# Key pages one step sooner, sample sums and offsets inside the projection steps, value products behind them, in a two-layer hybrid decoder step

## The chip, the cores and the metric

The kernel is one program on one core of a Trainium2 chip, written with an instruction stream of its own for each engine: TensorE (PE, products and transposes into PSUM), VectorE (DVE), ScalarE (ACT), GpSimd (POOL) and SyncE (SP, which requests most transfers). The streams run in order and meet in semaphores. The metric is the device time of one execution in microseconds; smaller is better.

## What is computed

The reference runs one inference step of a two-layer decoder on a prompt group (1 x 256 tokens) and a sample group (8 x 4 tokens), 288 token columns in all, with shared float32 weights and a model width of 1024:

```python
for l in range(DEPTH):                       # 2 layers
    m = silu(c) @ cond_w + cond_b            # 9 vectors per sequence: shift, scale, gate
    x = post(0, x, swiglu(pre(0, x), ffn_w_in[0], ffn_w_out[0]), 0.5)
    x = post(1, x, mixer(pre(1, x), ...), 1.0)
    x = post(2, x, swiglu(pre(2, x), ffn_w_in[1], ffn_w_out[1]), 0.5)

def mixer(a, ...):
    gq, gk, gv, gg, glr, mu, mv, sq, sk, sv = split_cols(a @ w_in)   # one projection, 3088 columns
    o_gla = gated linear attention (gates from the low-rank glr @ w2), 4 heads
    o_gm  = chunked spatial gating of mu, mv, 4 heads
    z     = q @ k^T * HD ** -0.5 + bias      # stick-breaking attention, 8 heads of 64
    A     = exp(log_sigmoid(z) + suffix sums of -softplus(z)), masked
    o_sb  = A @ v                            # samples: 1024 past keys and values in 8 pages of 128, through page_table
    return concat(o_gla, o_gm, o_sb) @ w_out
```

New keys, values and recurrent states are outputs too.

## The kernel before, in words

**Stages.** Per layer: feed-forward 0 (22 input steps, 16 output steps), a seam (norms, gates, residual), the mixer, a seam, feed-forward 1, a seam. A weight step brings 1 MB into one of two buffers `raw`; ScalarE rounds it (`w_hi`, L1325), VectorE takes the difference (`w_lo`, L1712), and TensorE forms three products for each 128 x 128 block with the 288 token columns (L605 to L607). A step's split into `w_hi` and `w_lo` waits until TensorE is done with the step two before it.

**Conditioning.** `cond_w` comes in chunks through the four buffers `direct` (and `side`); `cond_products` multiplies it into PSUM banks 6 and 7 with sequences on the partitions. VectorE copies the sums to `crow` (`copy_sums`, `copy_wide`), TensorE turns them back (`cond_turn`, L655), and VectorE makes scales, shifts and gates out of them (`modulation`), waiting for `cond_t`.

**Mixer, projection steps.** `MIX_STEPS` lists the twelve steps j = 0 to 11 (queries in 0 and 1, keys in 3 and 4). Beside them runs the scoring of the samples' past keys: 16 key chunks of four pages (1 MB each), requested by SyncE into `direct`, turned in 32 x 32 blocks by VectorE (`turn_keys`, L1990, 2 chunks a step), multiplied with the samples' queries by TensorE (`key_chunk`, L911, two chunks behind each of the steps 3 to 10, by `KEYS_AT`). The queries for that are repeated (`qrep`), transposed by TensorE (L1000), and laid out by VectorE (`sample_queries`). ScalarE brings the scores into `z` (`scores`), in two groups of four samples. Then, for each group g: cap (`sample_cap`; for group 1 GpSimd, L2354 and L2356), exp and log (`sample_log1p_exp`), sums (`sample_sums`, with totals at L2013 and L2014), offsets by small products (`part_offsets`) and their subtraction (`sample_offsets`), exp (`sample_weights`), a transpose (`turn_weights`), `regroup` on TensorE (L934), a copy into `a_keys` (`weights_by_page`). The low-rank gate product (L1017 to L1019) stands behind step 4.

**Mixer, tail.** Behind step 11: prompt scores, row transposes of keys and values, gated linear attention, spatial gating, prompt sums, and 16 value chunks (`value_chunk`, L957), 8 for each group, four buffers deep: SyncE requests chunk n when chunk n - 4 is used. The order of all this is written out by hand in each engine's stream. Then comes the output projection (first products L667).

Of the kernel before, what the change touches and what calls it, by code (L numbers as in the profile page):

```python
# [24 lines left out]
ALU = mybir.AluOpType  # L25
# [22 lines left out]
def decoder_step(nc, x_prompt, x_sample, c_prompt, c_sample, cache_sb_k, cache_sb_v, state_gla,  # L48
# [40 lines left out]
    KEYS_AT = {j: (2 * j - 6, 2 * j - 5) for j in range(3, 11)}  # L89
# [25 lines left out]
    with ctx:  # L115
# [60 lines left out]
        w2 = tile("w2", [LR, GW])  # L176
# [13 lines left out]
        lr = tile("lr", [LR, T])  # L190
# [13 lines left out]
        crow = tile("crow", [P, NCH // 2 * P], F32, shared + (2 * FB + 4) * T * 4)  # L204
# [22 lines left out]
        lrw_hi = tile("lrw_hi", [P, KB, P], F32R, crow_end)  # L227
        lrw_lo = tile("lrw_lo", [P, KB, P], F32R, crow_end + KB * P * 4)
        at[0] = crow_end + 2 * KB * P * 4
        lr_raw = tile("lr_raw", [P, KB, LR])  # L230
        qb = tile("qb", [P, 4, 4 * PR, 8, TS], F32, at[0])
        S0 = tile("S0", [P, B, GP, HD])
        att = tile("att", [P, 2, PT_, GP, P])
# [26 lines left out]
        direct_used = signal("direct_used", ND, 4 + NC0 + NSIDE)  # L260
        pages_in = signal("pages_in")
# [19 lines left out]
        cond_t = signal("cond_t", 3, 1)  # L281
# [23 lines left out]
        lrw_round = signal("lrw_round")  # L305
        lrw_ready = signal("lrw_ready")
# [98 lines left out]
        ROWS = 7  # L405
        TOKEN_BANKS = ((2, 3), (6, 7), (4, 0))
# [9 lines left out]
        def _(sp):  # L416
# [62 lines left out]
            def page_chunk(l, cache, dp, first, n, wait):  # L479

# [3 lines left out]
                room(l, dp, wait)  # L484
                for t, page in enumerate(found):
                    src = cache[l, ds(page, 1), :, :, :].rearrange("o s h d -> s (o h d)")
                    sp.dma_start(direct[:, n % 4, 512 * t:512 * t + 512], src).then_inc(direct_in[n % 4].sem, 16)  # L487

            def key_chunks(l, *chunks):
                for n in chunks:  # L490
                    page_chunk(l, cache_sb_k, DP_K, 4 * n, n, n)
# [58 lines left out]
            for l in range(L):  # L550
# [8 lines left out]
                mix_in(2, 3)  # L559
                key_chunks(l, 0, 1)  # L560
                mix_in(4)
                key_chunks(l, 2, 3)
                mix_in(5)
                for j in range(3, 9):
                    mix_in(j + 3)
                    key_chunks(l, *(n + 4 for n in KEYS_AT[j]))
                for n in range(NPC):
                    if n == 4:
                        for s in range(2):
                            mix(l, mix_w_out, POS_MO, s, s, s * 256)  # L570
                    page_chunk(l, cache_sb_v, DP_V, 4 * n, n, n)
# [26 lines left out]
        def _(pe):  # L598
# [11 lines left out]
            cond_sums = PS[:, 6:8, :].rearrange("p a b -> p (a b)")  # L610

# [116 lines left out]
            def ffn(l, n, cond_in):  # L728
# [32 lines left out]
                for s in range(N_IN - 4, N_IN):  # L761
                    in_step(l, n, s, s % 2)
                    if s == N_IN - 3:
                        turn_sums()
# [1667 lines left out]
```

## Time and profile before

| | |
|---|---|
| Time, median of 3 runs | 1382.98 us (1381.0 to 1384.24) |
| Profiled execution | time 1380.02 us, span 1378.3 us, mean granted clock 0.988 |
| TensorE busy | 1324.4 us, 96% |
| VectorE, ScalarE, GpSimd busy | 795.5 us (58%), 585.6 us (42%), 81.5 us (6%) |
| Read from HBM | 317.93 MB, 234 GB/s over the span |

The stretches of layer 0 are, in us from the start of the span: feed-forward 0 from 37 to 267, seam to 288, projection steps to 384, tail to 444, output projection to 472, seam to 486, feed-forward 1 to 706. Layer 1 follows with the mixer from 957 to 1114. Busy times overlap; an engine that isn't the bottleneck may idle at no cost.

### The profile page before, as it was taken

The page shows a single profiled execution, that of the slowest core. Times are in us where ns is not written, and L with a number is a line of the kernel's source. Part 1 is how long each engine was busy: PE and PEld are TensorE (multiplying, and loading weights), DVE is VectorE, ACT ScalarE, POOL GpSimd, SP SyncE. Part 2 cuts the span into 40 slices and gives each one's busy share as a digit, 9 for nine tenths or more (in the row PEclk, how much of TensorE's full clock was granted, in tenths as well). Part 3 has the DMA queues.
Part 4 walks back from the last instruction along what each step waited for, and adds up shares of the span by engine and source line. Part 5 has one row for each costly group of instructions (what it writes and reads, how often), then busy time and mean ns, then how long its engine had stood idle before and what let it go on. Part 6 is the DMA issues. An engine that isn't in the chain of part 4 may idle for free.

```text
span 1378.3 us, 34467 instructions
## 1 busy us (share of the span) xinstructions
PE 1324.4 (96%) x14014; PEld 1267.4 (92%) x14014; DVE 795.5 (58%) x1162; ACT 585.6 (42%) x965; POOL 81.5 (6%) x153
## 2 busy tenths in 40 slices
PE   6899999999989999999999999999998998999998
PEld 5899999999976899999989999998997787999998
DVE  2555553667884655554465555447788657555544
ACT  2532333443565543334353333345346555333343
POOL 4000000010040000000000000002003100000000
PEclk9999999999999999999999999999999998999999
DMA  9878779789989894658975566996997993565453
GB/s 330 266 231 259 219 244 311 219 257 327 298 274 343 256 324 140 168 154 270 282 239 156 161 174 195 289 276 199 329 342 228 338 326 101 156 174 158 136 168 97
DMA packets 423815, 324.49 MB, mean 235 GB/s; under 512 B 15559, under 2 KB 351719, under 8 KB 423696
## 3 DMA queue, kind: packets, MB, share of 16 engines
q1 hardware_dynamic: 421124, 317.03, 75.5%
q0 software_dynamic: 2272, 5.61, 1.2%
q8 instruction: 90, 1.47, 0.4%
q14 instruction: 29, 0.24, 0.1%
q10 hardware_dynamic: 300, 0.13, 0.0%
HBM read 317.93 MB, written 4.78 MB: 234 GB/s over the span
## 4 chain that ended last, share of the span: by engine, by line
PE 84%; DVE 5%; DMA 4%; SPq 3%; ACT 2%; issue 1%; DVEq 1%; POOL 0%; ACTq 0%
PE PS L605 23%; PE PS L607 23%; PE PS L606 23%; PE PS L633 3%; SPq L487 2%; PE PS L911 2%; PE PS L667 1%; PE PS L668 1%; PE PS L669 1%; DMA direct<-in_cond_w 1%; DMA direct<-in_cache_sb_v 1%; PE PS L957 1%; SPq L454 1%; DMA raw<-in_ffn_w_in 1%; DMA raw<-in_mix_w_in 1%
## 5 line engine op out<-in xcount | busy, mean ns | idle before, releaser
L1712 DVE TENSOR_TENSOR w_lo<-raw,w_hi 128x1024 fp32r<-128x1024 f32 (+1 forms) x368 | 392.9, 1106 | 445.9 <-ACT w_hi L1325 445.4
L1325 ACT ACTIVATE w_hi<-raw 128x1024 fp32r<-128x1024 f32 (+1 forms) x368 | 337.7, 960 | 657.6 <-PE PS L607 573.5
L605 PE MATMUL PS<-a_hi,w_hi 128*128 128x288 f32 x1760 | 524.0, 298 | 0.2 <-issue 0.2
L606 PE MATMUL PS<-a_lo,w_hi 128*128 128x288 f32 x1760 | 519.2, 295 | 0.0
L607 PE MATMUL PS<-a_hi,w_lo 128*128 128x288 f32 x1760 | 517.6, 294 | 0.0
L605 PEld LDWEIGHTS PS<-a_hi,w_hi 128*128 128x128 f32 x1760 | 329.7, 187 | 3.6 <-issue 3.3
L607 PEld LDWEIGHTS PS<-a_hi,w_lo 128*128 128x128 f32 x1760 | 331.4, 188 | 0.0
L606 PEld LDWEIGHTS PS<-a_lo,w_hi 128*128 128x128 f32 x1760 | 330.4, 188 | 0.5 <-issue 0.3
L606 PE MATMUL PS<-h_lo,w_hi 128*128 128x288 f32 x704 | 208.4, 296 | 0.0
L605 PE MATMUL PS<-h_hi,w_hi 128*128 128x288 f32 x704 | 208.1, 296 | 0.0
L607 PE MATMUL PS<-h_hi,w_lo 128*128 128x288 f32 x704 | 208.0, 296 | 0.0
L605 PEld LDWEIGHTS PS<-h_hi,w_hi 128*128 128x128 f32 x704 | 133.7, 190 | 0.4 <-issue 0.4
L607 PEld LDWEIGHTS PS<-h_hi,w_lo 128*128 128x128 f32 x704 | 132.0, 188 | 0.0
L606 PEld LDWEIGHTS PS<-h_lo,w_hi 128*128 128x128 f32 x704 | 131.9, 187 | 0.0
L633 PE MATMUL PS<-direct,cT 128*32 128x128 f32 x1920 | 66.0, 290 | 8.8 <-DMA direct<-in_cond_w 4.8
L1990 DVE STREAM_TRANSPOSE direct<-direct 128x2048 f32<-128x2048 f32 x32 | 72.2, 2289 | 0.0
L633 PEld LDWEIGHTS PS<-direct,cT 128*32 128x32 f32 x1920 | 55.1, 117 | 14.9 <-DMA direct<-in_cond_w 6.5
L2331 POOL TENSOR_TENSOR X<-X,Y 128x576 f32<-128x576 f32 x10 | 14.0, 1415 | 758.7 <-DVE Y L1798 758.7
L667 PE MATMUL PS<-a_hi,w_hi 128*128 128x288 f32 x160 | 50.0, 313 | 5.6 <-DVE a_lo L1961 5.6
L668 PE MATMUL PS<-a_lo,w_hi 128*128 128x288 f32 x160 | 48.1, 301 | 0.0
L669 PE MATMUL PS<-a_hi,w_lo 128*128 128x288 f32 x160 | 48.1, 300 | 0.0
L1863 DVE TENSOR_TENSOR h_lo<-hf,h_hi 128x288 f32 (+1 forms) x88 | 40.3, 458 | 11.7 <-issue 9.6
(327 smaller groups left out, 1160.1 us busy)
## 6 DMA issues: line engine op xcount, KB each, us to landing
raw<-in_ffn_w_in SPq DMA_DIRECT2D x176, 512.0 KB, 5.0
direct<-in_cond_w SPq DMA_DIRECT2D x240, 256.0 KB, 5.0
direct<-in_cache_sb_k SPq DMA_DIRECT2D x128, 256.0 KB, 4.4
direct<-in_cache_sb_v SPq DMA_DIRECT2D x128, 256.0 KB, 4.4
raw<-in_ffn_w_out SPq DMA_DIRECT2D x64, 384.0 KB, 3.8
raw<-in_mix_w_in SPq DMA_DIRECT2D x48, 512.0 KB, 6.9
raw<-in_ffn_w_out SPq DMA_DIRECT2D x64, 320.0 KB, 4.5
side<-in_cond_w SPq DMA_DIRECT2D x48, 256.0 KB, 5.3
```

Of the source, the lines that this page charges most:

```text
L487: sp.dma_start(direct[:, n % 4, 512 * t:512 * t + 512], src).then_inc(direct_in[n % 4].sem, 16)
L605: pe.matmul(out, whi, hi, start=begins and i == 0, stop=False)
L606: pe.matmul(out, whi, lo, start=False, stop=False)
L607: last = pe.matmul(out, wlo, hi, start=False, stop=ends and i == n - 1)
L633: last = pe.matmul(PS[32 * g:32 * g + 32, 6 + pair, c * P:c * P + P], cT[:, 4 * half + kb, :], rows[:, kb * 512 + g * P:kb * 512 + g * P + P],
L667: pe.matmul(out, whi, a_hi[:, k, :], start=k == 0, stop=False)
L668: pe.matmul(out, whi, a_lo[:, k, :], start=False, stop=False)
L669: last = pe.matmul(out, wlo, a_hi[:, k, :], start=False, stop=k == KB - 1)
L1325: act.activation(w_hi[:, s, at_:at_ + n], raw[:, s, at_:at_ + n], ACT.Copy)\
L1712: tt(w_lo[:, s, at_:at_ + n], raw[:, s, at_:at_ + n], w_hi[:, s, at_:at_ + n], ALU.subtract).then_inc(lo_done.sem, 1)
L1863: tt(h_lo[:, at_, :], hf[:, s:s + 1, :], h_hi[:, at_, :], ALU.subtract)\
L1990: dve.transpose(direct[:, n % 4, :], direct[:, n % 4, :]).then_inc(k_turned.sem, 1)
```

## The change

It has five parts. (1) Key chunks are requested, turned and multiplied one step sooner: chunks 0 and 1 stand behind step 2 and the last two behind step 9. The query transposes move between the two halves of step 2. (2) Sums of group 0 move from step 10 to step 8, its offsets to steps 9 and 10, its weights' transpose and the regrouping to step 11; the sums of group 1 come right behind the gate's scan, its offsets earlier too. ScalarE and TensorE do key rows inside steps 10 and 11. (3) Value chunks 0 to 7 each stand earlier in TensorE's stream, and every fifth one (`n % 5 == 4`) uses a new buffer `extra`. `S0` and `att` move onto parts of `Fm` and of the split buffers that are free by then; the load of `S0` waits for the last reads of the queries and keys there, and the seam for the state's output. (4) The products of `cond_w` take their columns in another order, so that VectorE's 32 x 32 transposes out of PSUM give the turned sums in `sums` directly; `crow`, `cond_turn`, `cond_t` and TensorE's waits for `mod_ready` go, and VectorE's loop over the first feed-forward's steps is unrolled. (5) The low-rank product takes unsplit weights of 32 columns in four column groups, summed by `w2`, repeated four times on the partitions.

```diff
-    KEYS_AT = {j: (2 * j - 6, 2 * j - 5) for j in range(3, 11)}
+    KEYS_AT = {j: (2 * j - 4, 2 * j - 3) for j in range(2, 10)}
...
+        extra = tile("extra", [P, 2048])
+        a_turn0 = tile("a_turn0", [P, 4 * NPG * 32], F32, at[0] - 8192)
+        S0 = tile("S0", [P, B, GP, HD], F32, shared + GQ * T * 4)
... sync
-                mix_in(2, 3)
+                mix_in(2)
                 key_chunks(l, 0, 1)
+                mix_in(3)
+                key_chunks(l, 2, 3)
                 mix_in(4)
-                key_chunks(l, 2, 3)
-                mix_in(5)
                 for j in range(3, 9):
-                    mix_in(j + 3)
-                    key_chunks(l, *(n + 4 for n in KEYS_AT[j]))
+                    mix_in(j + 2)
+                    key_chunks(l, 2 * j - 2, 2 * j - 1)
+                mix_in(11)
                 for n in range(NPC):
-                    if n == 4:
+                    if n % 5 == 4:
+                        extra_chunk(l, n)
+                    else:
+                        page_chunk(l, cache_sb_v, DP_V, 4 * n, n - (n + 1) // 5)
+                    if n == 3:
                         for s in range(2):
                             mix(l, mix_w_out, POS_MO, s, s, s * 256)
-                    page_chunk(l, cache_sb_v, DP_V, 4 * n, n, n)
... tensor
-                                         rows[:, kb * 512 + g * P:kb * 512 + g * P + P],
+                                         rows[:, kb * 512:kb * 512 + 512].rearrange("p (b g i) -> p g b i", g=4, i=32)[:, g],
...
-            def cond_turn(first=0, end=NCH // 2):
-
-                for q in range(first, end):
-                    last = pe.transpose(cond_sums[:, q * P:q * P + P], crow[:, q * P:q * P + P], ident[:, :])
-                last.then_inc(cond_t.sem, 1)
...
                             last = products(PS[:, 2 * s + h, 0:T], s, 1024 * h, a_hi, a_lo, 0, KB, True, True)
+                            if (j, h) == (2, 0):
+                                pe.wait_ge(cond_copied.sem, cond_copied.at(l, 12))
+                                pe.wait_ge(q_rep.sem, q_rep.at(l, 1))
+                                for p in range(PR):
+                                    turned = pe.transpose(PS[:, 6, p * P:p * P + P],
+                                                          qrep[:, p, :, :].rearrange("d a s -> d (a s)"), ident[:, :])
+                                turned.then_inc(q_t.sem, 1)
...
                     if j == 4:
-                        pe.wait_ge(lrw_ready.sem, lrw_ready.at(l, 1))
-                        for k in range(KB):
-                            pe.matmul(PS[:, 6, 0:T], lrw_hi[:, k, :], a_hi[:, k, :], start=k == 0, stop=False)
-                            pe.matmul(PS[:, 6, 0:T], lrw_hi[:, k, :], a_lo[:, k, :], start=False, stop=False)
-                            last = pe.matmul(PS[:, 6, 0:T], lrw_lo[:, k, :], a_hi[:, k, :], start=False, stop=k == KB - 1)
+                        for half in range(2):
+                            for part, src in enumerate((a_hi, a_lo)):
+                                for g in range(4):
+                                    k = 4 * half + g
+                                    last = pe.matmul(PS[32 * g:32 * g + 32, 6, 0:T], lr_raw[:, k, :],
+                                                     src[:, k, :].bitcast(F32), start=half + part == 0,
+                                                     stop=half + part == 2)
...
+                    if j == 9:
+                        pe.wait_ge(gate_x.sem, gate_x.at(l, 1))
+                        part_offsets(0, 7)
+                    if j == 10:
+                        rows_of(0, SK, 6, k_t)
+                    if j == 11:
+                        pe.wait_ge(mix_evac.sem, mix_evac.at(l, N_MI + 1))
+                        rows_of(1, SK, 0, k_t)
+                        rows_of(2, SK, 1, k_t)
+                        pe.wait_ge(z_got.sem, z_got.at(l, 5))
+                        pe.wait_ge(off_added.sem, off_added.at(l, 1))
+                        pe.wait_ge(kv_k.sem, kv_k.at(l, 1))
+                        regroup(0)
...
-                part_offsets(0, 7)
-                pe.wait_ge(mix_evac.sem, mix_evac.at(l, N_MI + 1))
+                pe.wait_ge(mix_evac.sem, mix_evac.at(l, N_MI + 2))
                 prompt_scores(0)
-                pe.wait_ge(mix_evac.sem, mix_evac.at(l, N_MI + 2))
+                pe.wait_ge(kv_k.sem, kv_k.at(l, 3))
                 prompt_scores(1)
                 pe.wait_ge(vn_f.sem, vn_f.at(l, 1))
+                pe.wait_ge(a_copied.sem, a_copied.at(l, 1))
...
+                value_chunk(0)
                 prompt_scores(2)
+                value_chunk(1)
                 prompt_scores(3)
... scalar, steps j = 10 and 11
                         act.activation(gt[1][:, :, :], gt[1][:, :, :], ACT.Ln, bias=1.0).then_inc(gate_l.sem, 1)
+                        scores(3)
+                        sample_weights(0)
                     if j == 11:
+                        sample_log1p_exp(1)
+                        key_rows(0, 6)
                         act.preload_act_table_set(SILU_TABLES)
                         act.activation(Fm[:, GG:GG + 2, :], Fm[:, GG:GG + 2, :], ACT.Silu)
                         act.preload_act_table_set(LOG_TABLES)
-                        scores(3)
                     mix_read(j)
...
+                weights_by_page(0)
+                key_rows(1, 0)
+                key_rows(2, 1)
                 act.wait_ge(gate_b.sem, gate_b.at(l, 1))
... vector
-                cp(crow[:, ds(i * 2 * P + (first + pair) * P, P)], PS[:, 6 + pair, 0:P]).then_inc(cond_copied.sem, 1)
+                own = sums[:, :, :].rearrange("p k c -> p (k c)")[:, ds(i * 2 * P + (first + pair) * P, P)]
+                dve.transpose(own, PS[:, 6 + pair, 0:P]).then_inc(cond_copied.sem, 1)
...
                 for j in range(N_MI):
                     if j == 1:
-                        dve.wait_ge(cond_t.sem, cond_t.at(l, 2))
                         own = lambda a, k: vec[:, a:a + k]
                         modulation(2, (1, own), own)
+                        turn_keys(0)
+                        turn_keys(1)
                     if j == 2:
                         dve.wait_ge(mix_evac.sem, mix_evac.at(l, 2 + 2))
                         cp(qrep[:, :, :, :], Fm[:, SQ:SQ + PR, NP:T].unsqueeze(2).to_broadcast([P, PR, 4, NS]))\
                             .then_inc(q_rep.sem, 1)
-                        turn_keys(0)
-                    if j == 3:
+                        turn_keys(2)
...
+                        sample_queries(1)
                     if j + 2 < N_MI:
                         split(l, POS_MI, j // 2 + 1, j % 2)
-                    if 3 <= j < 10:
-                        sample_queries(j - 2)
+                    if j == 2:
+                        turn_keys(3)
+                    if 3 <= j < 9:
+                        sample_queries(j - 1)
...
+                    if 3 <= j < 9:
+                        turn_keys(2 * j - 2)
+                        turn_keys(2 * j - 1)
+                    if j == 8:
+                        sample_sums(0)
...
                     if j == 10:
-                        sample_sums(0)
+                        sample_offsets(0, 7)
+                    if j == 11:
+                        turn_weights(0)
...
                 last.then_inc(gate_b.sem, 1)
+                sample_sums(1)
```

In the tail TensorE's new order is: prompt scores 0 and 1, the transposes of `dm`, value chunk 0, prompt scores 2, chunk 1, prompt scores 3, chunk 2, two row groups of the gated attention, the transpose of new weights, chunk 3, the third row group, `part_offsets(1, 5)`, then chunks 4 to 7 between the attention products, where chunks 2 to 5 stood; in front of `regroup(1)` no value chunk stands any more (before: 6 and 7).

## Rows read from the trace of the kernel before

**Rows 1.** Busy time by stretches (us, instructions), granted clock, DMA share, GB/s.
```profile
core 0: us, PE busy (x) PEld busy (x) DVE busy (x) ACT busy (x) POOL busy (x), PEclk, DMA share, GB/s
...
267.00:288.00 21.00, 18.29 (x463) 16.59 (x456) 17.20 (x35) 13.49 (x33) 8.28 (x9) 1.00 0.54 158
288.00:383.00 95.00, 94.56 (x1143) 89.94 (x1142) 74.65 (x67) 39.76 (x56) 2.21 (x2) 1.00 1.02 318
383.00:446.00 63.00, 56.62 (x982) 42.78 (x981) 43.51 (x76) 37.54 (x82) 16.99 (x21) 0.97 0.91 307
...
486.00:706.00 220.00, 219.89 (x1806) 218.43 (x1802) 112.11 (x172) 82.74 (x121) 0.00 (x0) 0.99 0.74 217
```

**Rows 2.** Waits on TensorE, 288.2 to 444.7, first and last of 8: total, times, longest.
```profile
PE PS L957 <- DMA direct<-in_cache_sb_v: 2.2, 2, 1.6
...
PE PS L911 <- DVE direct L1990: 0.3, 1, 0.3
```

**Rows 3.** The same for layer 1, 957.2 to 1114, first and last of 11.
```profile
PE PS L957 <- DMA direct<-in_cache_sb_v: 2.6, 3, 1.3
...
PE PS L605 <- issue: 0.2, 1, 0.2
```

**Rows 4.** Busy time in one stretch of each layer's tail, columns as in Rows 1.
```profile
393.50:398.40 4.90, 4.33 (x49) 2.71 (x50) 4.00 (x8) 4.83 (x12) 3.38 (x5) 0.65 0.43 113
1063.10:1067.80 4.70, 3.04 (x49) 1.80 (x49) 4.44 (x8) 4.63 (x12) 4.46 (x7) 1.00 0.25 66
```

**Rows 5.** Timeline of TensorE: start, us, what; a turn of sums, the low-rank product.
```profile
180.65 0.81 PE L655 MATMUL PS<-ident,crow 128*128 128x128 f32 x6
181.22 0.38 PE L605 MATMUL PS<-a_hi,w_hi 128*128 128x288 f32 x1
...
320.69 0.40 PE L1017 MATMUL PS<-a_hi,lrw_hi 128*128 128x288 f32 x1
...
323.98 0.29 PE L605 MATMUL PS<-a_hi,w_hi 128*128 128x288 f32 x1
```

**Rows 6.** The chain that ended last, in order of time: two conditioning chunks.
```profile
59.58 1.88 PE PS L633 x64
```

**Rows 7.** Timeline of SyncE's requests, layer 0's mixer.
```profile
289.15 4.32 SPq L487 DMA_DIRECT2D direct<-in_cache_sb_k  x8
...
399.68 37.10 SPq L487 DMA_DIRECT2D direct<-in_cache_sb_v  x48
```

**Rows 8.** Timeline of VectorE, steps 0 to 2 of layer 0 (idle before in brackets).
```profile
289.53 2.36 DVE L1712 TENSOR_TENSOR w_lo<-raw,w_hi 128x1024 fp32r<-128x1024 f32 x2 [1.67 <-ACT w_hi L1325]
...
298.87 0.42 DVE L2045 COPY qrep<-Fm 128x512 f32<-128x512 f32 x1
```

**Rows 9.** Timeline of TensorE: query transposes, keys behind step 8, first value chunks.
```profile
301.63 0.60 PE L1000 MATMUL PS<-ident,qrep 128*128 128x128 f32 x4
...
357.43 2.15 PE L911 MATMUL PS<-direct,qb 128*32 128x128 f32 x64
...
398.40 1.96 PE L957 MATMUL PS<-direct,a_keys 128*32 128x128 f32 x64 [0.56 <-ACT a_keys L1497]
```

**Rows 10.** Timeline of VectorE: split, key transposes, sums of group 0.
```profile
358.68 2.36 DVE L1712 TENSOR_TENSOR w_lo<-raw,w_hi 128x1024 fp32r<-128x1024 f32 x2 [0.24 <-ACT w_hi L1325]
...
362.23 4.50 DVE L1990 STREAM_TRANSPOSE direct<-direct 128x2048 f32<-128x2048 f32 x2
...
377.02 1.20 DVE L2004 TENSOR_TENSOR sm<-sm,z 128x1040 f32<-128x1040 f32 x1
...
380.99 0.17 DVE L2014 COPY new_totals<-sm 128x4 f32<-128x4 f32 x1
```

**Rows 11.** Timeline of GpSimd: the cap of group 1 in both layers.
```profile
386.42 2.86 POOL L2356 TENSOR_SCALAR sm<-z 128x1040 f32<-128x1040 f32 x1 [0.61 <-issue]
...
1057.36 2.85 POOL L2356 TENSOR_SCALAR sm<-z 128x1040 f32<-128x1040 f32 x1 [1.99 <-issue]
```

**Rows 12.** Timeline of ScalarE: table load, SiLU, exp of group 1.
```profile
376.52 1.28 ACT L1544 ACT_TABLE_LOAD   x1
377.81 0.69 ACT L1545 ACTIVATE Fm<-Fm 128x576 f32<-128x576 f32 x1
...
393.94 1.10 ACT L1484 ACTIVATE sm<-sm 128x1040 f32<-128x1040 f32 x1
```

More of the change, by code:

```diff
@@ L405, in decoder_step @@
         ROWS = 7
+        SMALL = 7
         TOKEN_BANKS = ((2, 3), (6, 7), (4, 0))
@@ L477, in cond, with page_table_entries @@
                     cond_load(L - 1, c * D - D, slot)
-            def page_chunk(l, cache, dp, first, n, wait):
+            def page_table_entries(first):
                 _, found = nc.values_load_multi_w_load_instructions(
@@ L797, in filled_seam @@
             def filled_seam(l, seam, x, dp, first, middle, end, layer):
-                if first == 0:
-                    pe.wait_ge(mod_ready.sem, mod_ready.at(layer, x))
                 cond_chunk(layer, x, dp, *divmod(first, 4))
@@ L950, in value_chunk @@
                             pe.wait_ge(o_rows_got.sem, o_rows_got.at(l, g))
-                        else:
-                            pe.wait_ge(kv_k.sem, kv_k.at(l, 3))
-                    k = direct_in[n % 4]
-                    pe.wait_ge(k.sem, k.at(l, DP_V // 4 + 1 + n // 4) * 64)
+                    d = n - (n + 1) // 5
+                    if n % 5 == 4:
+                        rows, done, by = extra[:, :], extra_used, 1
+                        pe.wait_ge(extra_in.sem, extra_in.at(l, n // 5 + 1) * 64)
+                    else:
+                        rows, done, by = direct[:, d % 4, :], direct_used, 1 if n < NPC - 1 else 4
+                        k = direct_in[d % 4]
+                        pe.wait_ge(k.sem, k.at(l, DP_V // 4 + 1 + d // 4) * 64)
+                    if n == NPC - 1:
+                        for slot in range(1, 4):
+                            pe.sem_inc(direct_in[slot].sem, 64)
                     for t in range(4):
@@ L977, in turn_rows, with rows_of @@
                     last.then_inc(o_turned.sem, 1)
+                def rows_of(i, f0, bank, done):
+                    sl, n = token_tile(i)
+                    for p in range(PR):
+                        last = pe.transpose(PS[0:n, bank, p * P:p * P + P], Fm[:, f0 + p, sl], ident[:, :])
+                    last.then_inc(done.sem, 1)
                 for j in range(N_MI):
@@ L1075, in prompt_values @@
                     last.then_inc(op_sum.sem, 1)
-                def rows_of(i, f0, bank, done):
-                    sl, n = token_tile(i)
-                    for p in range(PR):
-                        last = pe.transpose(PS[0:n, bank, p * P:p * P + P], Fm[:, f0 + p, sl], ident[:, :])
-                    last.then_inc(done.sem, 1)
                 def gla_rows(i, bank):
@@ L1525, in _ @@
                         sample_log1p_exp(0)
+                        scores(2)
                     if j == 9:
@@ L1868, in ffn @@
                 if n == 0 and l == 0:
-                    with dve.Fori(0, NCH // 4) as i:
+                    for i in range(NCH // 4):
                         for s in range(6):
```

194 lines of the change are left out of this document (84 added, 110 removed).

## The prediction

> **What bounds the kernel now.** I read the table by stretches first. In the feed-forward stretches TensorE is busy throughout (219.89 of 220 us) while the DMA share is 0.74 [rows 1]: there only TensorE work counts. In the twelve projection steps of the mixer TensorE has 94.56 of 95 us and the DMA share is 1.02: both are full. The rest of the mixer (I call it the tail) is the place with holes: 56.62 of 63 us busy in layer 0 [rows 1]. The lists of waits on TensorE over both parts of the mixer say what they are: 8 kinds of wait, 6.8 us together, in layer 0 and 11 kinds, 8.1 us, in layer 1; the largest in both is a value page not yet landed (2.2 and 2.6 us) [rows 2, 3], the others are single waits of 0.2 to 1.2 us for VectorE, ScalarE and GpSimd. Two things are hidden in "busy". A product counts as busy until its modelled end, so each wait costs about 0.2 us more than its row says (layer 0: 9 waits, 1.8 us; layer 1: 13, 2.6 us). And layer 0 has a stretch at a granted clock of 0.65, the same 49 instructions that layer 1 does at 1.00 [rows 4]: TensorE is busy 4.33 us against 3.04, so 1.3 us are lost to the lower level (1.2 instead of 2.4 GHz). It came after the holes of 0.7, 0.7 and 1.1 us. What the tail loses today: 6.8 + 1.8 + 1.3 = 9.9 us in layer 0, 8.1 + 2.6 = 10.7 in layer 1.
>
> **What is certain to go.** (a) The turns of conditioning sums. Six transposes hold the next product back from 180.65 to 181.22, 0.57 us [rows 5]. Three such turns and one of two transposes stand in feed-forward stretches where nothing else waits: 3 x 0.57 + 0.2 = 1.9 us. The first (four transposes) stands ahead of the first weights, which set that start; I count 0. The two in the mixer are in (b). VectorE's transposes replace its own copies of the same size, at the same place and beside TensorE's products, so they cost the path nothing new; the unrolled loop on VectorE issues the same instructions as before. (b) In each mixer: a turn, 0.57; and the low-rank product. That runs from 320.69 to 323.98, 3.3 us for 24 products [rows 5]. The new one is 16 full-precision products of 288 columns into four column groups. The nearest row is the conditioning chunk: 32 such products (64 records) of 128 columns in 1.88 us, 0.059 us each [rows 6]; for 288 columns 0.132, so 2.1 us. Saved 1.2. Together 1.8 us per layer.
>
> **DMA.** Key pages 0 and 1 were requested only at 289.15 [rows 7], behind the weights of step 3, whose buffer comes free with the last split of step 1. Now they stand ahead of those weights, their own buffers are free some 5 to 10 us sooner, and the DMA share from 267 to 288 is only 0.54 [rows 1]. Later weights stand behind no more bytes than before, except those of step 3, which are needed late. In the tail SyncE spends 399.68 to 436.78 on twelve value chunks, 3.1 us each [rows 7], because the first chunk of values is used at 398.4 [rows 9]; afterwards the first use is some 3 us earlier, four more chunks are used before it would matter, and there is a fifth buffer. I expect no wait for a value page: 2.2 and 2.6 us go (they are in the 9.9 and 10.7).
>
> **What the new order makes TensorE wait for**, from the durations above, on the clock of layer 0.
> 1. The query transposes now stand between the halves of step 2 and wait for the copy of the queries. VectorE's row now: split of step 2 ends 291.9 [rows 8], modulation ends about 292.7; then come two key transposes (4.5 us, [rows 10]) until 297.2, the split of step 3 (2.3) until 299.5, the copy (0.4) until 299.95 [rows 8]. Step 1 begins 0.6 earlier than before, so the first half of step 2 ends at 301.63 [rows 9] - 0.6 - 3.2 = 297.8. Wait: 2.3 us. Before, the copy was done 2.3 us before it was wanted.
> 2. Totals. Step 8 ends at 357.4 (T) [rows 9]. VectorE then does split (to T+3.7), queries and mean (T+4.9), two key transposes (T+9.3) and the sums up to the totals, 377.02 to 381.15, 4.15 us: T+13.5 [rows 10]. TensorE has keys 2.1, gate 1.2, step 9 6.5, keys 1.9: T+11.7. Wait: 1.9 us; it stood after step 11, unseen, and a wait for a key transpose (0.3) leaves.
> 3. Behind step 11 TensorE needs step 11's evacuation. ScalarE's line is now: gate exp/log to T+19.9, GpSimd's subtraction to T+21.4, its mask and cap (0.8 + 2.86 [rows 11]) to T+25.1, exp and log of 1040 columns (2 x 1.1 [rows 12]) to T+27.4, key rows 0.6, then two table loads and a SiLU (1.28 + 0.69 + 1.28 [rows 12]) to T+31.2, evacuation T+31.9. TensorE: T+13.6, offsets 0.7, steps 10 and 11 with key rows 13.6, two more key rows and the regrouping 1.8: T+29.7. Wait: 2.2 us. Then ScalarE copies keys before it frees banks: 1.3 us more.
> 4. Small ones: the transposed decays (0.4), the masked weights (1.2), the group-1 chain without value chunks 6 and 7 in front of it (1.7 + 0.7), two waits that are there today and stay (0.4 + 0.4), and 0.5 on a key transpose.
> Sum: 2.3 + 1.9 + 2.2 + 1.3 + 0.4 + 1.2 + 2.4 + 0.8 + 0.5 = 13.0 us per layer, all measured from TensorE's own pace.
>
> **The sum.** Layer 0: 13.0 - 9.9 - 1.8 = +1.3. Layer 1: 13.0 - 10.7 - 1.8 = +0.5. Feed-forward: -1.9. Together -0.1, and since in a chain of waits a longer one partly shortens the next I take -0.5 us. The profiled execution has a span of 1378.3 us and a time of 1380.02; that becomes 1379.5, and the median of the three runs, 1382.98, becomes 1382.5.
>
> **One rule weighed.** GpSimd's cap is on the path of wait 3. In layer 0 it started 0.61 us after the mask was added, in layer 1 1.99 us [rows 11], beside VectorE's work. The Trainium skill, "SBUF — State Buffer", Terms, says that VectorE and GpSimd share a port pair that is locked for a whole instruction, and that the loser blocks fully. By that rule the sum would be that of the third rival below; the row of layer 1 is as the rule has it, the one of layer 0 less so.
>
> **Rivals.**
> - *Forecast, the waits change places* (within 0.2%, that is 2.8 us, about what a measurement of this kernel can tell from no change). Chance 0.40.
> - *The tail closes up.* If ScalarE's and VectorE's lines start earlier than I put them (the first values need no DMA, the sums are a whole step earlier), waits 3 and 4 go and only 1 and 2 stay: 4.2 + 1.2 per layer instead of 13.0 would be -15.3; if half of that comes, -7.5: 1375. For it: the longest waits of the list go for certain. Against it: ScalarE's order has GpSimd's cap in front of the last evacuation. Chance of over 0.2% faster by this or by a smaller wait 1: 0.33.
> - *GpSimd's cap is held up by VectorE* (the other side). In the new order it runs at T+22 to T+25 beside VectorE's scans and differences with two inputs in SBUF, 2.2 us together. If it starts 2.0 us late as in layer 1, or is blocked throughout, wait 3 grows by 1.4 to 2.2 per layer: +2.8 to +4.4; it decides from 1.6 us per layer on: 1386. For it: the 1.99 us row. Against it: the cap itself has the same 2.85 us in both layers. With the wait of 2.3 in a dense stretch the clock may also fall once more (1.3 us). Chance 0.24. By that page of the Trainium skill this would be the likely case.
> - *The column groups of the low-rank product don't run side by side at 288 columns*: 4 x 2.1 = 8.4 against 3.3 us, +5.1 and the lost 1.2, per layer +6.3: 1395. The conditioning rows speak against it. Chance 0.03.
>
> **Range.** The first rival's half and the second's full price give 1375 and 1387; the unknown of wait 3 and one fall of the clock more add 2: 1375 to 1389. Faster 0.33, same 0.40, slower 0.27.
>
> **What would show it.** A new wait of about 2.3 us on TensorE at the query transposes and 1.9 us at the offsets of group 0; the wait for the last evacuation in front of the first prompt scores; no wait for value pages; low-rank product 2.1 us; no transposes of conditioning sums. I am wrong if the query copy is earlier than half of step 2, if ScalarE gets its cap sooner, or if value pages are still late.

## The result and the profile after

The changed kernel takes 1396.07 us (median of 6 runs, 1390.14 to 1399.52), the kernel before beside it 1382.88. The ratio of the runs is 1.0084, 95% interval 1.0064 to 1.0104: slower, where 1382.5 was forecast, and outside the range of 1375 to 1389. The profiled execution took 1396.48 us with a span of 1394.7 and a mean granted clock of 0.984.

Where the 16.4 us between the two spans lie is read from TensorE's timeline, each stage taken from its first product to the first product of the next. In us, before and after:

| stage | before | after | difference |
|---|---|---|---|
| feed-forward, four stretches | 873.5 | 870.5 | -3.0 |
| mixer, layer 0 / layer 1 | 162.9 / 163.3 | 163.1 / 169.8 | +0.2 / +6.4 |
| output projection, layer 0 / layer 1 | 26.5 / 26.5 | 31.6 / 32.3 | +5.1 / +5.8 |
| seams, five together | 75.6 | 77.3 | +1.8 |

The busy times by stretches of the kernel after, columns as in [rows 1], which they answer to; the last two are the output projections:

```profile
287.80:384.00 96.20, 92.35 (x1138) 87.53 (x1137) 78.66 (x71) 37.42 (x56) 5.25 (x4) 0.98 1.02 317
384.00:444.50 60.50, 55.15 (x979) 41.91 (x978) 38.75 (x70) 38.85 (x83) 14.60 (x18) 1.00 0.73 248
444.50:476.10 31.60, 28.43 (x199) 27.61 (x199) 14.69 (x20) 13.06 (x24) 1.81 (x2) 0.95 0.94 282
1124.20:1156.50 32.30, 28.41 (x198) 27.60 (x199) 14.65 (x20) 13.06 (x24) 1.82 (x2) 0.95 0.99 291
```

The output projections of the kernel before, same view:

```profile
444.60:471.10 26.50, 26.48 (x200) 26.06 (x196) 14.16 (x20) 13.07 (x24) 1.81 (x2) 1.00 0.94 282
1113.90:1140.40 26.50, 26.48 (x201) 26.07 (x197) 14.20 (x20) 13.07 (x24) 1.82 (x2) 1.00 0.95 285
```

The same 200 instructions, once without a hole and once with 3.2 us of holes and a clock of 0.95. The forecast has no term there. What they wait for is found on SyncE. First its requests in the kernel after, then in the kernel before:

```profile
431.37 1.88 SPq L505 DMA_DIRECT2D extra<-in_cache_sb_v  x4
433.75 2.33 SPq L494 DMA_DIRECT2D direct<-in_cache_sb_v  x4
443.34 3.75 SPq L455 DMA_DIRECT2D direct<-in_cond_w  x8
447.13 3.48 SPq L426 DMA_DIRECT2D raw<-in_mix_w_out  x2
```

```profile
429.92 6.86 SPq L487 DMA_DIRECT2D direct<-in_cache_sb_v  x11
437.38 3.66 SPq L454 DMA_DIRECT2D direct<-in_cond_w  x8
442.82 1.35 SPq L425 DMA_DIRECT2D raw<-in_mix_w_out  x2
```

The conditioning chunks of the seam are requested 6.0 us later and the weights of output step 2, which stand behind them, 4.3 us later. ScalarE, which rounds these weights, after and before; the brackets are its idle time:

```profile
456.44 1.06 ACT L1339 ACTIVATE w_hi<-raw 128x1024 fp32r<-128x1024 f32 x1 [6.25 <-DMA raw<-in_mix_w_out]
465.43 1.06 ACT L1339 ACTIVATE w_hi<-raw 128x1024 fp32r<-128x1024 f32 x1 [4.97 <-DMA raw<-in_mix_w_out]
```

```profile
452.09 2.01 ACT L1325 ACTIVATE w_hi<-raw 128x1024 fp32r<-128x1024 f32 x2 [2.03 <-PE PS L669]
460.46 1.06 ACT L1325 ACTIVATE w_hi<-raw 128x1024 fp32r<-128x1024 f32 x1 [5.14 <-DMA raw<-in_mix_w_out]
```

Before, step 2 waited for TensorE alone; after, it waits for the transfer, 4.35 us later.

Within the mixer, TensorE's waits in layer 0 (five of eight) and in layer 1 (the longest of nine), answering to [rows 2, 3]:

```profile
PE PS L1012 <- DVE qrep L2062: 1.9, 1, 1.9
PE PS L923 <- DVE new_totals L2028: 1.9, 1, 1.9
PE PS L945 <- DVE wst L2158: 1.3, 1, 1.3
PE PS L1080 <- ACT Fm L1486: 1.1, 1, 1.1
PE PS L1080 <- ACT kst L1517: 1.1, 1, 1.1
```

```profile
PE PS L1080 <- ACT Fm L1486: 2.6, 1, 2.6
```

The waits for the queries and the totals are 1.9 us each in layer 1 too. No value page is waited for any more. All together 9.0 us in layer 0 and 11.1 in layer 1 (each with a last one of 0.2 at the first output product). In layer 1 the granted clock also fell in three stretches:

```profile
970.60:978.00 7.40, 5.46 (x30) 5.25 (x29) 5.98 (x7) 0.00 (x0) 0.00 (x0) 0.77 0.99 259
1061.00:1073.00 12.00, 8.32 (x99) 5.92 (x99) 7.87 (x14) 8.97 (x18) 4.03 (x4) 0.72 0.29 91
1093.00:1103.00 10.00, 8.76 (x152) 6.09 (x148) 3.76 (x7) 1.69 (x3) 0.00 (x0) 0.83 0.87 304
```

The first holds the wait for the queries, the second the two for ScalarE. In layer 0 the clock fell once, to a mean of 0.90 over 374 to 388, behind the wait for the totals.

### The profile page after: what moved, and what is told of

It reads as the page before. It is cut to its first block, busy times and chain, and to the rows that moved or that the text cites. A ratio compares the mean times of both kernels' runs of the same rounds, so it can differ in the third digit from the quotient of the medians.

```text
span 1394.7 us, 34340 instructions
## 1 busy us (share of the span) xinstructions
PE 1326.4 (95%) x13994; PEld 1267.8 (91%) x13994; DVE 797.2 (57%) x1160; ACT 584.0 (42%) x963; POOL 84.2 (6%) x158
## 4 chain that ended last, share of the span: by engine, by line
PE 78%; issue 9%; ACT 3%; SPq 3%; DMA 3%; DVE 2%; POOL 1%; ACTq 0%; DVEq 0%; POOLq 0%
PE PS L628 21%; PE PS L629 20%; PE PS L630 20%; PE PS L654 4%; SPq L455 2%; PE PS L967 2%; PE PS L682 1%; PE PS L684 1%; PE PS L683 1%; DMA raw<-in_mix_w_out 1%; PE PS L1089 1%; PE PS L912 1%; DMA raw<-in_ffn_w_in 1%; DVE direct L2004 1%; DMA xtok<-in_x_sample 1%
## 5 line engine op out<-in xcount | busy, mean ns | idle before, releaser
L1881 DVE TENSOR_TENSOR h_lo<-hf,h_hi 128x288 fp32r<-128x288 f32 (+1 forms) x88 | 40.3, 458 | 9.9 <-issue 6.4
```

The costliest lines, as they stand in the source:

```text
L1881: tt(h_lo[:, at_, :], hf[:, s:s + 1, :], h_hi[:, at_, :], ALU.subtract)\
```

## Experiments

Times are medians; "less" and "more" compare with the kernel before in the same session (1382.0 to 1383.6), intervals are those of the ratio.

**1. The weights requested first.** On SyncE, in the changed kernel:

```diff
                 for s in range(2):
-                    cond_seam(l, 0, 2 * s, 2 * s + 2)
                     mix(l, mix_w_out, POS_MO, 2 + s, s, (2 + s) * 256)
+                    cond_seam(l, 0, 2 * s, 2 * s + 2)
```

> The changed kernel, with SyncE requesting the weights of output steps 2 and 3 ahead of the conditioning chunks beside them instead of behind them. Theory A (request order): the first conditioning chunk now waits for the last value chunk (requested at 443.34, before 437.38) and the weights of output step 2 stand behind it (447.13, before 442.82); the output projection takes 31.6 and 32.3 us instead of 26.5 and 26.5. Then with this order the weights are requested at about 443.2, no wait for w_lo is left in the output projection, it takes 26.5 us in both layers, and the time falls by 10 to 11 us against the changed kernel: about 1385.5, ratio to the kernel before 1.002. Rival B (the transfers themselves are late because the queue is fuller at the end of the tail): the request comes earlier, the landing does not, and the time stays within 3 us of 1396.

1389.02 us, 6.7 more (1.0032 to 1.0076). About half of the loss goes. The output projection takes 28.4 and 28.8 us: ScalarE's rounding for step 2 waits for TensorE again and not for the transfer, no wait for `w_lo` is left, and the products themselves are through after 26.8 and 26.5 us, but now there is a hole right behind them. SyncE, ScalarE and TensorE of this kernel:

```profile
455.10 8.04 SPq L455 DMA_DIRECT2D direct<-in_cond_w  x8
463.19 6.95 SPq L426 DMA_DIRECT2D raw<-in_ffn_w_in  x4
```

```profile
470.33 1.06 ACT L1339 ACTIVATE w_hi<-raw 128x1024 fp32r<-128x1024 f32 x1 [5.01 <-DMA raw<-in_ffn_w_in]
473.05 0.64 ACT L1699 ACTIVATE Y<-PS 128x576 f32<-128x576 f32 x1
```

```profile
475.31 0.46 PE L692 MATMUL PS<-yacc,ones 128*32 128x72 f32 x16 [1.60 <-DVE yacc L2257]
```

The lateness was only handed on: the next weights in the queue are requested at 463.2 (before 455.6), and ScalarE has their rounding in front of an evacuation that the end of the projection needs.

**2. Only the late request, in the kernel before.**

```diff
+                sp.wait_ge(direct_used.sem, direct_used.at(l, DP_C[0]))
                 for s in range(2):
                     cond_seam(l, 0, 2 * s, 2 * s + 2)
```

> The kernel before, with one wait added on SyncE: the conditioning chunks behind the mixer are requested only when the last value chunk has been used. Theory A: this alone, with nothing else of the change, puts 5 us into each output projection, so the time rises by 9 to 11 us to about 1393, ratio 1.007. Rival B (late landing belongs to the other parts of the change): under 3 us more.

1396.73 us, 14.4 more (1.0084 to 1.0128): with nothing else of the change, the whole of its loss. The output projections:

```profile
446.50:478.00 31.50, 28.51 (x204) 27.66 (x201) 14.39 (x20) 13.20 (x24) 1.82 (x2) 0.95 0.94 284
1118.30:1152.60 34.30, 29.61 (x200) 28.84 (x196) 14.35 (x20) 13.17 (x24) 1.82 (x2) 0.90 1.00 291
```

The price was underrated (5.0 and 7.9 us in this profile): behind the hole the clock falls too, to a mean of 0.90 over the projection in layer 1.

**3. Requests by the buffer that is really free.** Value chunk n is number n - (n + 1) // 5 of the four `direct` buffers, so the last one (15) is number 12 and lies in buffer 0, which is the first conditioning chunk's. Buffers 1 and 2 are free after value chunks 11 and 12.

```diff
-                for s in range(2):
-                    cond_seam(l, 0, 2 * s, 2 * s + 2)
-                    mix(l, mix_w_out, POS_MO, 2 + s, s, (2 + s) * 256)
+                for s in (1, 2):
+                    sp.wait_ge(direct_used.sem, direct_used.at(l, DP_V + 9 + s))
+                    cond_load(l, 8 * D, s)
+                mix(l, mix_w_out, POS_MO, 2, 0, 2 * 256)
+                sp.wait_ge(direct_used.sem, direct_used.at(l, DP_V + 12))
+                cond_load(l, 8 * D, 3)
+                cond_seam(l, 0, 0, 1)
+                mix(l, mix_w_out, POS_MO, 3, 1, 3 * 256)
```

> The changed kernel, with the conditioning chunks behind the mixer requested by the buffer that is really free: chunks 1 and 2 (their buffers are last used by value chunks 11 and 12) ahead of the weights of output step 2, then chunk 3 and chunk 0 (whose buffer the last value chunk holds), then the weights of output step 3. Theory A, refined after e1_weights_first (there the output projection still took 28.4 and 28.8 us: the weights of the feed-forward were now requested at 463.2 instead of 455.6 in the kernel before, and ScalarE, whose stream has their split in front of the last evacuation, held back the end by 1.6 us): with nothing late in the ring the output projection takes 26.5 us in both layers, 4.2 us less than e1_weights_first, so about 1385. If the ring isn't the whole of it, 1387 to 1389.

1384.04 us, 2.0 more (1.0003 to 1.0032). The output projections, layer 0 and 1:

```profile
446.60:473.40 26.80, 26.44 (x198) 26.07 (x198) 14.61 (x20) 13.01 (x24) 1.82 (x2) 1.00 0.87 266
1117.30:1143.80 26.50, 26.48 (x200) 26.09 (x196) 14.28 (x20) 13.08 (x24) 1.82 (x2) 1.00 0.97 295
```

This reordering of the requests for four conditioning chunks turns 13.2 us more into 2.0 us more (each against the kernel before in its session), so it is worth some 11 us. What is left of the change costs 0.4 to 4.4 us by the interval, not far from the -0.5 that was forecast of the whole. All kernels from number 6 on contain it.

**4. The two parts that need no new order, in the kernel before.** `crow` becomes `sums`, VectorE transposes into it, `cond_turn` and `mod_ready` waits go; the low-rank product as in the change; nothing else.

> The kernel before with only the two parts that need no new order: sums of conditioning turned by VectorE (no products of TensorE for it), and the low-rank product with unsplit weights in four column groups. By the prediction's terms: 1.9 us in the feed-forward stretches and 1.8 us in each mixer, 5.5 us in all, so about 1377.4, ratio 0.996. Rival: VectorE's unrolled loop or the strided operand costs something in the feed-forward stretches (they measured -0.65, -1.45, -0.65, -0.2 us in the changed kernel), and the low-rank gain is taken back by the later wait for value pages: 1380 to 1383.

1378.39 us, 4.0 less (0.9959 to 0.9989), of 5.5 forecast, which this interval (1.5 to 5.7 us) includes. Beside the 2.0 us more of number 3 it says that the new order of parts 1 to 3 by itself costs some 6 us, if the parts add up; the forecast had it cost 5.4 (13.0 - 9.9 and 13.0 - 10.7). In its profile the mixers took 161.5 and 162.6 us (before 162.9 and 163.3), feed-forward 1 of layer 0 216.4 (before 217.8, some 0.8 of which was a start at the lower clock).

**5. Query transposes behind the second half of step 2,** with the order of requests of number 1.

```diff
-                            if (j, h) == (2, 0):
+                            if (j, h) == (2, 1):
```

> The order of requests as in e1_weights_first, and the query transposes of TensorE behind the second half of step 2 instead of between its halves. If wait 1 (1.94 us in each layer) is only its own length, it goes and nothing takes its place up to step 9: 3.9 us less than e1_weights_first. If the half clock after it in layer 1 (granted clock 0.77 over 970.6 to 978.0) also comes from that hole, up to 1.7 us more goes: 4 to 6 us less. Rival: VectorE has the layout of the queries 3 us later then, the key products wait for that instead, and less than 2 us goes.

1388.00 us, 5.6 more (1.0028 to 1.0057), 1 us less than number 1, which two intervals this wide can't tell from nothing. The rival holds: the wait for `qrep` is gone and has a new place, in both layers.

```profile
PE PS L912 <- DVE qb L1998: 1.5, 1, 1.5
```

**6. ScalarE: table loads and SiLU ahead of exp and log of group 1.**

```diff
-                        sample_log1p_exp(1)
                         key_rows(0, 6)
                         ... SiLU with its two table loads
+                        sample_log1p_exp(1)
```

> As e5_ring_order, and on ScalarE the two table loads and the SiLU stand in front of exp and log of group 1 instead of behind them, so that they fill the 2.0 us in which ScalarE waits for GpSimd's cap. Step 3 of the prediction: the evacuation of step 11 ends ScalarE's line and TensorE waits for it (1.1 us in layer 0, 2.6 in layer 1), then for the keys' copies (1.1 and 1.1). Both waits should go: 2.2 to 3.7 us per layer, 4 to 6 us less than e5_ring_order. Rival: VectorE's sums of group 1 start 1.4 us later by it and a wait further down (the new weights' transpose, the second regrouping) grows by as much: 0 to 2 us less.

1384.70 us, 2.7 more (0.9999 to 1.0032), no gain on number 3. The wait for the evacuation is gone and 1.5 us each for a key copy and the masked weights stand instead: the rival.

**7. TensorE's three moves alone,** on number 3: offsets of group 0 between the halves of step 10, query transposes behind step 2, first key chunks between the halves of step 3.

```diff
+                            if (j, h) == (10, 0):
+                                pe.wait_ge(gate_x.sem, gate_x.at(l, 1))
+                                part_offsets(0, 7)
+                            if (j, h) == (3, 0):
+                                for n in KEYS_AT[2]:
+                                    key_chunk(n)
...
-                            if (j, h) == (2, 0):
+                            if (j, h) == (2, 1):
```

> As e5_ring_order, with only TensorE's three moves of e7_no_waits (offsets between the halves of step 10, query transposes behind step 2, first key chunks between the halves of step 3), ScalarE's order as in the changed kernel. By the forecast's steps 1 and 2 the two waits of 1.9 us per layer go, 7.6 us less than e5_ring_order, 1376.5. Since ScalarE's line ends at the evacuation of step 11 and TensorE now comes to it 1.9 us sooner, the rival has half of that come back as a wait there: 3 to 5 us less, 1379 to 1381.

1385.67 us, 2.1 more (0.9999 to 1.0028): nothing gained, less than even the rival had. Both waits of 1.9 us are gone in both layers, and the list of layer 0 begins with this one, followed by one of 1.4 us put down to "issue":

```profile
PE PS L1088 <- ACT Fm L1494: 3.1, 1, 3.1
```

and the stretch behind step 11 has lost its clock:

```profile
388.00:400.00 12.00, 8.59 (x82) 6.48 (x86) 7.19 (x15) 7.82 (x17) 5.20 (x6) 0.57 0.37 108
```

The clock alone can hold up to (1 - 0.57) x 12 = 5.2 us there, more than the two waits of the layer.

**8. Both together,** the edits of 6 and 7.

> As e6_act_order, and on TensorE the offset products of group 0 between the halves of step 10 (3.2 us later than now), the query transposes behind step 2 and the first two key chunks between the halves of step 3. Steps 1 and 2 of the prediction (1.9 us each, in both layers) go: 7.6 us. If the falls of the granted clock behind them (0.90 over 374 to 388 in layer 0, 0.77 over 970.6 to 978 in layer 1, 1.2 to 1.7 us of work each) come from these holes, up to 3 us more: 8 to 10 us less than e6_act_order. Rival: the offsets being later pushes ScalarE's weights of group 0 and with them the line that ends at the evacuation of step 11, and half of it comes back as a wait there.

1377.43 us, 4.6 less (0.9952 to 0.9978), 7.3 less than number 6. Each edit alone gave nothing, both give 7. TensorE's line and ScalarE's run side by side into the same point, the evacuation of step 11. Counted from the first product of the mixer it begins, in layer 0 and 1, at

| kernel | layer 0 | layer 1 |
|---|---|---|
| number 3 | 108.6 us | 108.5 us |
| number 7, TensorE's moves alone | 106.7 | 107.2 |
| number 6, ScalarE's order alone | 108.7 | 106.7 |
| both | 103.3 | 104.3 |

Of the 108.7 of number 6 some 2 us are a stretch with a granted clock of 0.69 in step 2. So each edit alone moved this point by 1.3 to 1.9 us, and lost it again behind it: number 6 in longer waits for a key copy and the masked weights (1.5 us each, from 1.1 and 1.3) and new small ones, number 7 in the clock. How much of the 7 us is the two lines and how much the clock isn't separated.

**9. The gate first on VectorE,** on number 8: its two operations and the offsets of group 0 ahead of the split of step 11; key rows ahead of the regrouped weights on ScalarE.

```diff
+                    if j == 9:
+                        ... the gate's two operations, moved up
+                        sample_offsets(0, 7)
                     if j + 2 < N_MI:
                         split(l, POS_MI, j // 2 + 1, j % 2)
```

> As e7_no_waits, and on VectorE the gate's two operations and the offsets of group 0 stand ahead of the split of step 11 instead of behind it, and on ScalarE the copies of key rows 1 and 2 ahead of those of the regrouped weights. What ends last behind step 11 is a chain: gate difference on VectorE (376.3 in e7_no_waits, though its input is there at 371.5) - exp and log (ScalarE idle 4.0 us ahead of it) - mask and cap on GpSimd - exp and log of group 1 - evacuation of step 11. If that chain is what TensorE waits for (1.2 and 1.1 us in layer 0, 2.2 and 1.1 in layer 1), 2 to 3 us come off it, both waits go, VectorE's sums of group 1 and what is behind them come 2 us sooner: 4 to 6 us less than e7_no_waits, about 1372. Rival: the time is set further down (the masked weights, 1.1 us, the chain of the second group), and the waits only move there: under 2 us less.

1376.10 us, 7.5 less (0.9917 to 0.9958). That is 2.9 us more than number 8 gained, of 4 to 6 forecast, and the two intervals overlap, as they do for number 12: a gain on number 8 isn't shown. The chain hardly became shorter, because GpSimd's operations now stand beside VectorE's split. GpSimd's subtraction in number 8, then the same with the mask behind it and VectorE's second `w_lo` of the split in number 9:

```profile
378.62 1.43 POOL L2380 TENSOR_TENSOR gt<-gt,gt 128x576 f32<-128x576 f32 x1 [51.76 <-ACT gt L1570]
```

```profile
375.63 2.00 POOL L2379 TENSOR_TENSOR gt<-gt,gt 128x576 f32<-128x576 f32 x1 [50.64 <-ACT gt L1570]
376.26 2.46 DVE L1736 TENSOR_TENSOR w_lo<-raw,w_hi 128x1024 fp32r<-128x1024 f32 x1
377.60 1.19 POOL L2384 TENSOR_TENSOR z<-z,new_mask 128x16 f32<-128x16 f32 x1
```

In number 8 the mask took 0.21 us and a `w_lo` 1.23. The times here fit operations that stand still until the other engine's is over: the first `w_lo` ends at 376.34 and the subtraction 1.29 us behind it, the second `w_lo` 1.09 us behind the subtraction, the mask 0.07 us behind that. Counted from the mixer's first product the gate's difference on VectorE comes 2.1 us sooner than in number 8 (mean of the layers), the cap only 0.5; the 1.55 us between are those that GpSimd's two operations grew by. By the listed waits the wait for the evacuation is down to 0.8 and 0.2 us, and one of 2.5 us stands behind it.

**10. The same without ScalarE's orders.**

> As e8_gate_first, with ScalarE's order of the changed kernel (exp and log of group 1 ahead of the SiLU, regrouped weights ahead of key rows). The chain starts 2.4 us sooner, so that the SiLU between the log and the evacuation costs less: the wait for the evacuation should be under 1 us, within 2 us of e8_gate_first. If ScalarE's order matters (3.2 us of table loads and SiLU on the chain), 2 to 5 us more than e8_gate_first.

1382.63 us, 0.9 less (0.9980 to 1.0006), 6.5 us more than number 9: ScalarE's order matters. The wait for the evacuation is 3.1 us in both layers, not under 1.

**11. Masks of the prompt scores ahead of the sums of group 1,** on number 9, whose longest wait in each layer was this:

```profile
PE PS L1088 <- ACT zp L1591: 2.5, 1, 2.5
```

```diff
                 last.then_inc(gate_b.sem, 1)
-                sample_sums(1)
...
                 prompt_scores(1)
+                sample_sums(1)
```

> As e8_gate_first, and on VectorE the masks of prompt scores 0 and 1 (two pairs of 0.83 us) ahead of the sums of group 1 (384.8 to 390.1), which are now what TensorE waits for in front of prompt scores 2 (2.5 us in both layers). The sums end 1.7 us later and are wanted by the offset products of group 1 only some 8 us behind. The 2.5 us go in both layers: 3 to 5 us less than e8_gate_first, about 1371. Rival: the later sums and with them the turned weights and the second regrouping are late now, and the wait moves to the masked weights or to the second group: under 2 us less.

1382.12 us, 0.2 less (0.9971 to 1.0002): 6.8 us more than number 12 beside it. Its longest wait, and the stretch behind it:

```profile
PE PS L1118 <- DVE vn L2159: 4.8, 1, 4.8
```

```profile
400.00:415.00 15.00, 14.66 (x206) 11.55 (x205) 10.47 (x23) 10.16 (x24) 3.05 (x5) 0.69 0.84 274
```

The rival was right that the wait moves, too mild in price, and named other places: VectorE copies `vn` behind the sums, no sooner than in number 9, and TensorE now only comes to it earlier. The scans of the sums also ran beside GpSimd's product this time and took almost twice as long, in number 9 and here:

```profile
386.09 2.44 DVE L2030 TENSOR_TENSOR_SCAN sm<-ones,sm 128x256 f32<-128x256 f32 x4
```

```profile
390.09 4.65 DVE L2030 TENSOR_TENSOR_SCAN sm<-ones,sm 128x256 f32<-128x256 f32 x4
```

Counted from the mixer's first product (layer 0) TensorE gets past the hole at 116.1 us, and past the same point at 116.3 in number 9, so nothing is lost up to there. The loss comes behind it: over the next 15 us the granted clock is 0.69, against 1.00 in number 9; in layer 1 it is 0.69 over 16.5 us.

**12. Number 9 again,** beside number 11.

> The kernel of e8_gate_first once more, beside e10_scores_first on the same chip, to have their difference free of the chip's own: ratio 0.994 to the kernel before as in its first run (0.9917 to 0.9958).

1375.30 us, 7.0 less (0.9937 to 0.9970). Number 9 beats the kernel before in two sessions.

## Why the prediction was wrong

**The step that failed** is in the paragraph on DMA: "Later weights stand behind no more bytes than before". Bytes were counted, not waits, and so the sum has no term for the output projections. `cond_seam` asks for a buffer by a number that was numbered anew: before, the first conditioning chunk waited for value chunk 12, now it waits for 15, because four buffers carry 13 chunks and the last falls into buffer 0. The output weights stand behind this request in SyncE's stream, so the queue passes the delay on. The step cost 10.9 us in the profile and some 11 us in the medians (13.2 us more than the kernel before, 2.0 us more with the requests mended). Experiment 2 shows it alone, 3 takes it away alone, and 1 shows that the order within the queue, not the transfer, is the cause. TensorE's four waits in the output projection of layer 0 (2.1, 0.8, 0.3 and 0.2 us) name `w_lo`, an evacuation and `a_lo`, none the load of `S0` or the state's output.

**Point by point.**
- *Conditioning turns*, -1.9 us: the four feed-forward stretches gave -3.0, with 0.8 from the start at half clock in the profile before: -2.2.
- *Low-rank product*, 3.3 to 2.1: right. It now runs from 323.28 to 325.33, and the rival that column groups don't run side by side falls, though its 1395 was nearest to the time:

```profile
323.28 0.67 PE L1033 MATMUL PS<-a_hi,lr_raw 128*32 128x288 f32 x8
...
325.33 0.40 PE L628 MATMUL PS<-a_hi,w_hi 128*128 128x288 f32 x1
```

 The two certain parts by themselves gave 4.0 us of 5.5 (experiment 4).
- *Value pages*: right. Their waits went, 2.2 and 2.6 us.
- *Wait 1*, 2.3: measured 1.9 in both layers; the copy of the queries began at 298.97, forecast 299.55. The forecast's own numbers give 299.95 - 297.8 = 2.15, not 2.3. *Wait 2*, 1.9: 1.9 in both.
- *Wait 3*, 2.2 and then 1.3: 1.1 and 1.1 in layer 0, 2.6 and 1.1 in layer 1. Its mechanism stands as written, ScalarE's line behind GpSimd's cap, in the changed kernel:

```profile
377.07 0.69 ACT L1560 ACTIVATE gt<-gt 128x576 f32<-128x576 f32 x1 [4.02 <-DVE gt L2095]
383.95 1.07 ACT L1497 ACTIVATE sm<-sm 128x1040 f32<-128x1040 f32 x1 [2.06 <-POOL sm L2379]
386.67 1.28 ACT L1568 ACT_TABLE_LOAD   x1
...
389.94 0.65 ACT L1486 ACTIVATE Fm<-PS 128x576 f32<-128x576 f32 x1
390.49 1.21 ACT L1511 ACTIVATE a_keys<-PS 128x256 f32<-128x256 f32 x4
```

- *Small waits*, 5.3 us in the sum: 3.0 us came in layer 0 (9.0 in all, less 1.9, 1.9, 1.1 and 1.1). The masked weights had 1.3 for 1.2; the group-1 chain's 1.7 and 0.7 didn't come. With the prediction's own 0.2 us on top of each wait the two lists come to 10.8 us (9 waits) and 13.1 (10 waits), against 13.0: in sum the waits of layer 0 were priced 2 us too high, those of layer 1 right.
- *The mixers*: forecast +1.3 and +0.5, measured +0.2 and +6.4. What is missing in layer 1 is the clock: by the stretches above, as an estimate, its three falls can hold at most (1 - 0.77) x 7.4 + (1 - 0.72) x 12 + (1 - 0.83) x 10 = 6.8 us, for which the sum has no term; the prediction put one fall of 1.3 us into its range. In the profiles of experiments 1, 3 and 5, which leave the mixer's order as it is but for the query transposes in 5, layer 1 takes +1.9, +2.3 and +3.1 us, so that most of the 6.4 belongs to that one execution. The six runs of the changed kernel scatter over 9.4 us, with a mean granted clock of 0.987 in the shortest and 0.979 and 0.983 in the two longest; the share of each hole isn't settled.
- *The sum over waits* treated them as terms to be added. Experiments 6 to 8 show that they are not: waits 1 and 2 (7.6 us over two layers) taken away gave nothing while ScalarE's line was as late, and 7 us once it was shortened as well. That the two lines meet is shown; that nothing came at all in 7 is in part the clock's doing.
- *GpSimd's cap held up by VectorE*: didn't come; it was VectorE that was held up. The cap began 0.85 us after the mask (0.83 in layer 1) and took its usual time. The first scan of the gate on VectorE, with two inputs in SBUF, began 0.28 us after it. That scan in the kernel before, where GpSimd stood idle, then in the changed kernel with the cap:

```profile
382.37 0.76 DVE L2081 TENSOR_TENSOR_SCAN gt<-restart,gt 128x288 f32<-128x288 f32 x1
```

```profile
381.06 2.86 POOL L2379 TENSOR_SCALAR sm<-z 128x1040 f32<-128x1040 f32 x1 [0.85 <-issue]
381.34 1.38 DVE L2104 TENSOR_TENSOR_SCAN gt<-restart,gt 128x288 f32<-128x288 f32 x1
```

 By the rule of the Trainium skill, "SBUF — State Buffer", Terms, the two engines share a port pair that is held for the full instruction, and the loser fully blocks. The trace agrees in part: the scan lost 0.62 us, but the second one took its usual 0.72 us beside the same cap. The operations with two inputs on both engines in experiment 9 do wait for each other's ends.
- *The tail closes up*: it could, but not by this change. Experiment 9 has its -7.5 us, with the requests mended, three moves on TensorE and another order on ScalarE, without which 6.5 us of it are missing (experiment 10).

Open: the seams took 1.8 us more, with five "issue" waits of up to 1.5 us among TensorE's conditioning products against three before. They come at other places in each run and also in experiment 4, and no experiment was made on them.

## What to carry to other kernels

When a ring of buffers is numbered anew, list for every request behind it which use it now waits for, and then for every request queued behind that one; the order of four chunks' requests was worth more than the rest of the change. Where two engines' lines run into one point, a wait taken from one can give nothing until the other is shorter too: look for what bounds both before adding up waits. A longest wait in a list is a place to look, not a price: taking 2.5 us away in experiment 11 cost 6.8. And an operation that is moved on one engine gets other neighbours: where VectorE's and GpSimd's operations came to stand side by side, in experiments 9 and 11, operations grew to up to twice their length and more.

## What was not expected of the hardware

Holes in dense stretches of TensorE can cost more than their length, because the granted clock falls to a mean of 0.57 to 0.90 over the 7 to 34 us around or behind them: 0.77 with a hole of 1.9 us, 0.57 with holes of 3.1 and 1.4, 0.69 behind one of 4.8, 0.90 over the output projection of layer 1 in experiment 2. It doesn't always fall: in the changed kernel the hole of 1.9 us at the queries left 1.00 in layer 0 and 0.77 in layer 1, and the one at the totals 0.90 in layer 0 and 1.00 in layer 1.

VectorE and GpSimd can hold each other up: a `w_lo` of 128x1024 took 2.46 us instead of 1.23 and a mask of 128x16 on GpSimd 1.19 instead of 0.21 (experiment 9), four scans 4.65 instead of 2.44 (experiment 11).

Full-precision products of 288 columns run side by side in four column groups, as forecast: 16 in 2.05 us.
